# A mixture-of-experts kernel whose expert lists go from 96 slots to 128, in an order that goes around sixteen groups of partitions

## The reference

```python
def expert_block(args):
    tok, e = args
    xb = x_pad[tok]
    hb = jax.nn.silu(xb @ w_gate[e]) * (xb @ w_up[e])
    return hb @ w_down[e]
...
yb = yb.reshape(n_rows, dm) * row_w[:, None].astype(yb.dtype)
routed = jax.ops.segment_sum(yb, row_tok, num_segments=n_tok + 1)[:n_tok]
```

## Time and profile before

| | |
|---|---|
| median of 3 runs | 1192.11 us (1189.66 to 1192.6) |
| the profiled execution | 1189.86 us, its span 1188.1 us, mean granted clock 0.98 |
| PE busy (weight loads apart) | 94% of the span |
| PEld, DVE, ACT, POOL busy | 71%, 71%, 58%, 27% |
| experts | from about 450 to 1090 us of the span |
| DMA engines in that stretch | busy share at the top digit, 355 to 375 GB/s in most slices |
| DRAM traffic | 275 MB read, 36 MB written |

### The profile page before, as it was taken

One profiled execution on the slowest core, in us unless ns is written; L12 is line 12 of the kernel. 1 busy time (PEld: TensorE's weight loads), 2 busy tenths in 40 slices (PEclk: granted clock), 3 DMA queues, 4 the chain that ended last, 5 costly groups with the idle time before them and its releaser, 6 DMA issues.

```text
span 1188.1 us, 15715 instructions
## 1 busy us (share of the span) xinstructions
PE 1120.9 (94%) x5390; PEld 843.3 (71%) x5390; DVE 846.1 (71%) x1034; ACT 688.6 (58%) x692; POOL 326.0 (27%) x183
## 2 busy tenths in 40 slices
PE   2999999998999889999999999999999999999896
PEld 2878877777878665777777776767777777667475
DVE  7454345453444575999999988988989998887376
ACT  4431234342232432887888887777878887777344
POOL 4000000000002432444444443433444443331431
PEclk9999999998989999999999999999999999999899
DMA  7532222113234536999999999999999999998721
GB/s 284 169 105 71 71 71 70 38 36 142 73 118 175 211 111 233 348 365 373 368 375 368 368 369 355 364 357 353 363 364 358 370 371 358 363 363 266 244 110 54
DMA packets 68475, 294.78 MB, mean 248 GB/s; under 512 B 11216, under 2 KB 14288, under 8 KB 43600
## 3 DMA queue, kind: packets, MB, share of 16 engines
q1 hardware_dynamic: 52944, 256.43, 57.3%
q0 software_dynamic: 14912, 35.68, 12.2%
q10 hardware_dynamic: 576, 2.10, 0.5%
HBM read 275.29 MB, written 35.65 MB: 262 GB/s over the span
## 4 chain that ended last, share of the span: by engine, by line
PE 37%; DMA 16%; DVE 6%; ACT 3%; issue 3%; DVEq 0%; ACTq 0%; POOLq 0%; SPq 0%
DMA gu_raw<-in_moe_w_up 13%; PE ps L400 10%; PE ps L402 10%; PE ps L401 10%; PE ps L1454 3%; DVE w_lo L1653 2%; ACT w_hi L1545 2%; PE ps L1908 1%; PE ps L1194 1%; DMA gu_raw<-in_moe_w_gate 1%; DMA residual_rows<-y,put_idx 1%; DMA odd_rows<-y,put_idx 1%; PE ps L1478 1%; DVE w_lo L384 1%; PE ps L1445 1%
## 5 line engine op out<-in xcount | busy, mean ns | idle before, releaser
L1653 DVE TENSOR_TENSOR w_lo<-gu_raw,w_hi 128x2048 fp32r<-128x2048 f32 x126 | 288.5, 2290 | 52.0 <-ACT w_hi L1545 51.4
L1545 ACT ACTIVATE w_hi<-gu_raw 128x2048 fp32r<-128x2048 f32 x128 | 242.6, 1913 | 55.1 <-DMA gu_raw<-in_moe_w_up 42.9
L400 PE MATMUL ps<-w_hi,xgT_hi 128*96 128x512 f32 x512 | 205.9, 402 | 5.9 <-issue 3.2
L1756 POOL DMA_INDIRECT xg<-h_rows,get_idx x64 | 154.5, 2414 | 206.0 <-DVE get_idx L1641 156.5
L402 PE MATMUL ps<-w_hi,xgT_lo 128*96 128x512 f32 x512 | 202.9, 396 | 0.0
L401 PE MATMUL ps<-w_lo,xgT_hi 128*96 128x512 f32 x512 | 201.7, 394 | 0.0
L400 PE MATMUL ps<-w_hi,act_hi 128*128 128x512 f32 x384 | 156.4, 407 | 5.3 <-PEq L494 2.8
L401 PE MATMUL ps<-w_lo,act_hi 128*128 128x512 f32 x384 | 151.5, 394 | 0.0
L402 PE MATMUL ps<-w_hi,act_lo 128*128 128x512 f32 x384 | 151.4, 394 | 0.0
L1658 DVE TENSOR_TENSOR dn_lo<-dn_raw,dn_hi 128x2048 fp32r<-128x2048 f32 x64 | 146.0, 2282 | 4.3 <-ACT dn_hi L1551 4.1
L280 POOL TENSOR_TENSOR x_rows<-x_rows,ln_b 128x1024 f32<-128x1024 f32 x10 | 23.8, 2377 | 401.3 <-DVE x_rows L273 401.3
(11 more groups left out here) (201 smaller groups left out, 1740.6 us busy)
## 6 DMA issues: line engine op xcount, KB each, us to landing
gu_raw<-in_moe_w_gate SPq DMA_DIRECT2D x64, 1024.0 KB, 15.0
gu_raw<-in_moe_w_up SPq DMA_DIRECT2D x64, 1024.0 KB, 14.8
dn_raw<-in_moe_w_down SPq DMA_DIRECT2D x64, 1024.0 KB, 14.7
raw<-in_w_in SPq DMA_DIRECT2D x18, 1024.0 KB, 5.1
h_rows<-x_rows SPq DMA_DIRECT2D x8, 512.0 KB, 4.7
raw<-in_w_out SPq DMA_DIRECT2D x4, 1024.0 KB, 5.6
ple_raw<-in_ple_w_gate SPq DMA_DIRECT2D x4, 1024.0 KB, 10.5
x_rows<-in_x SPq DMA_DIRECT2D x4, 512.0 KB, 6.6
```

The costliest lines, as they stand in the source:

```text
L400: nc.tensor.matmul(out, x_hi, w_hi, start=first, stop=False)
L1545: nc.scalar.activation(m.w_hi[:, 2 * x.b + half], m.gu_raw[:, 2 * x.b + half], ACT.Copy).then_inc(gu_hi, 1)
L1653: nc.vector.tensor_tensor(m.w_lo[:, 2 * x.b + half], m.gu_raw[:, 2 * x.b + half], m.w_hi[:, 2 * x.b + half].bitcast(F32), ALU.subtract).th ...
L1756: nc.gpsimd.indirect_dma_start(out=m.xg[x.q][0:CAP], out_offset=None, in_=h1, in_offset=bass.IndirectOffsetOnAxis(ap=m.get_idx[x.q][0:CAP] ...
```

## The change

The list gets 128 slots, so that it covers all partitions. The `iota` into `slots` becomes two, which give another order: partition p = 64h + 32u + 4g + v (h, u of 0 and 1, g of 0 to 7, v of 0 to 3) holds the place 8h + g + 16u + 32v. The eight partitions that share h and g are one of sixteen groups; group 8h+g holds the places 8h+g, 8h+g+16, and so on. Two tiles move, because with 128 columns for each block they are larger: `hT_lo` to 110 KiB, `onehot` to 181 KiB. The number of rounds that the slots could need falls from 6 to 4; one is run either way.

```diff
-SLOTS = 96
+SLOTS = 128
 FAR = 4096.0
-QUEUES = 16
...
-        self.hT_lo = at("hT_lo", [P, 2, 2 * cap], F32R, 181)
+        self.hT_lo = at("hT_lo", [P, 2, 2 * cap], F32R, 110)
...
-        self.onehot = at("onehot", [P, 2, NT, cap], BF16, 182.5)
+        self.onehot = at("onehot", [P, 2, NT, cap], BF16, 181)
...
-    nc.gpsimd.iota(m.slots[:, 0:rounds * cap].rearrange("p (r q j) -> p r q j", r=rounds, q=QUEUES),
-                   pattern=[[cap, rounds], [1, QUEUES], [QUEUES, cap // QUEUES]], base=0, channel_multiplier=0,
-                   allow_small_or_imprecise_dtypes=True)
+    parts = m.slots[:, 0:rounds * cap].rearrange("p (r h u g v) -> p r h u g v", r=rounds, h=2, u=2, g=8)
+    for u in range(2):
+        nc.gpsimd.iota(parts[:, :, :, u], pattern=[[cap, rounds], [8, 2], [1, 8], [32, 4]], base=16 * u,
+                       channel_multiplier=0, allow_small_or_imprecise_dtypes=True)
```

## The result

The changed kernel takes 1199.23 us (median of 4 runs, 1198.66 to 1203.69) against 1191.23 us for the kernel before in the same comparison: ratio 1.0076, 95% interval 1.0047 to 1.0104. In a second comparison it came to 1.0099 (1.0064 to 1.0135). It is slower; the forecast was 1187.4 us, and faster. The profiled execution of after took 1203.69 us, its span 1202.0 us.

A forecast was written before the change was run, and what follows sets the result against it. The prediction took the engines to bound the early experts and the weight transfers the late ones. Early steps +3.2 us, late ones -8.9 and single items +1.0 gave -4.7, so 1187.4 us, range 1179 to 1200.

The forecast's parts named there:

- GpSimd: Making the transfer lists: at most 0.42 us more for 32 slots, hidden for gathers and counted as nothing for scatters.
- the cover: Slack before put_idx on DVE needs the scatter landed: step 0.14 us longer, put_idx about 0.4 us later in it.
- sign of being wrong: At put_idx on DVE: waits growing beyond some 5 us would show the prediction wrong.
- the scatter's lists: Rival, chance 0.05: GpSimd's delay grows, scatters land after put_idx wants them, 0.4 us in 60 steps, 1211 us.
- The transfers don't gain: Rival, chance 0.17: slow weight packets beside gathers come from two streams meeting, not from partitions; 1199 us.
- The transfers' relief: Expert weights and gathers on the DMA engines: 0.50 us less per expert, 0.03 us back for empty slots.
- The engines' pace: PE, DVE and ACT loop in the expert stage: 9.92 us a step, 0.14 more than 9.78.
- the engines take it all: Rival, chance 0.20: PE's matmul spacing stays at 0.232 us, engine pace 9.98 us a step, 1191.4 us.
- weight loads show: Rival, chance 0.03: 36 PE weight loads at +30 ns in the open, +1.1 us a step, 1252 us.
- The sum: Whole kernel: early steps +3.2 us, late ones -8.9, single items +1.0, together -4.7 us.

The follow-up runs named there:

- after_put4: The changed kernel with four put_idx tiles instead of two, so put_idx waits for the scatter of four experts back: 1179.92 us, ratio 0.9919 to the kernel before.
- after_same_chip: The changed kernel run once more, unaltered, beside the follow-up kernels on one chip: 1201.26 us, ratio 1.0099 to the kernel before.
- blocks128: The changed kernel with its 128 slots in the old kind of order, eight neighbouring partitions to a block: 1252.77 us, ratio 1.0543 to the kernel before.
- cols128: The kernel before, lists of 96 in the old order, with xgT, hT, onehot and their conversions 128 wide: ratio 1.0020.
- list128: The changed kernel's lists of 128 in the new order, but products, transposes and conversions for 96 columns: ratio 0.9974 to the kernel before.
- list128_put4: The changed kernel with products, transposes and conversions for 96 columns and four put_idx tiles: 1174.66 us, ratio 0.9877 to the kernel before.
- scat96: The changed kernel with put_idx and the scatter over partitions 0 to 95 alone, the gather keeping 128: ratio 0.9940 to the kernel before.

## Why the prediction was wrong, step by step

- **The step that failed is "GpSimd".** It had the right place and even the right wait, which it put at nothing, and its bound, "up to 0.4 us a step", is what the wait cost: 0.33 us early and 0.45 late, 19 to 21 us in all by the medians. Two terms were mis-sized. The landing was to go from 9.1 to 9.5 us; it is 10.1 at the median and 13.1 at worst in after_put4, and 10.7 and 13.3 in after_same_chip. Only the time in which GpSimd makes the list was priced there, and the way of the further slots through the DMA engines at 0.03 us, as a share of bandwidth. The packet records show the reverse: the time to the first packet stayed (5.2 and 5.1 us), and the packets' own stretch grew from 3.6 to 4.8. The other term is the cover, 0.14 and about 0.4 us: it grew by 0.2. And both were medians, while the latest landings went from 10.6 to 13.3 and 14.0 us, and a DVE wait is made by the late ones. A zero that rests on a cover of the same size as the cost was no zero. The prediction's own sign of being wrong, waits of `put_idx` beyond some 5 us, came: 26.1.
- **The rival that came true** had a chance of 0.05: the scatter's lists, with `put_idx` waiting. Its condition was that GpSimd's delay to the first packet grows, and that did not happen. Its result, 1211 us, is the forecast of 1187.4 with 0.4 us in 60 steps on top, 24 us. The wait cost 19 to 21, and what it stood on was lower than forecast (below).
- **The number 1199 stands in the prediction, by another rival.** "The transfers don't gain" (0.17) gave 1199 us, and 1199.23 was measured. That is luck: the transfers did gain, and a wait that this rival does not have took the gain back. The stated range, 1179 to 1200, holds the result for the same reason, and on the slower side.
- **The transfers' relief was right in kind and smaller than forecast**: 42.4 us of waits of ACT went. In the late windows the queues took of the sixteen engines, first before (692.1 to 1060.1 us), then in after_put4 (695.8 to 1053.2 us):

```profile
q1 hardware_dynamic: 15665, 114.10, 80.6%
q0 software_dynamic: 8064, 19.07, 21.4%
```

```profile
q1 hardware_dynamic: 15533, 113.11, 79.7%
q0 software_dynamic: 10368, 19.08, 21.4%
```

  Times the steps of 10.22 and 9.93 us, that is 10.43 and 10.04 us of all engines an expert, 0.39 us of relief, and 0.3 when the 0.9% more weight bytes in the first window are taken out; 0.50 - 0.03 was forecast. The rows of gathers fell to 159 ns as forecast (161). By blocks128 the relief needs the new order too, which the rows of the prediction could not tell. The gather's instruction on POOL is 0.39 us longer (2806 ns against 2414), hidden as forecast.
- **The engines' pace was right.** `onehot` 691 ns, `xgT_lo` 1218 ns in the rows above (0.69 and 1.21 forecast); without the wait the early steps take 9.91 us (9.92), the late ones 9.93 (9.98). PE's matmuls in the expert stage of after (738.10 to 742.42, 19 spacings) start 0.227 us apart:

```profile
738.10 0.39 PE L401 MATMUL ps<-w_lo,xgT_hi 128*128 128x512 f32 x1
...
742.42 0.40 PE L402 MATMUL ps<-w_hi,xgT_lo 128*128 128x512 f32 x1
```

  and not at 0.232 as in the earlier trace rows, in spite of the wider weight loads. The prediction left open whether the width or the load around it does that. It goes with the width: from 500 to 1060 us the spacings of these matmuls average 231.7 ns in before, cols128 and also list128 and list128_put4, which have the new transfers and 96 columns, and 228.0 to 228.2 in after, after_put4, blocks128 and scat96. Over 36 matmuls that is 0.13 us (0.12 taken). The rivals "the engines take it all" and "weight loads show" are out.
- **The sum** of -4.7 us, less the wait, was too small: after_put4 has -9.6 us (0.81% of 1190) where the same steps gave -4.7. The late steps at 9.93 in place of 9.98 account for 1.9 us of it; the other 3.0 stand against an interval of 2.3 us either way. In the profiles 2.7 us of it lie behind the late window (128.0 us before, 125.3 in after_put4, to the end of the span), where the prediction had +0.1; why is open.

## What to carry to other kernels

An empty slot of a transfer by list was cheap here in bandwidth and dear in latency: 32 more of them in a scatter added 0.8 us from its first packet to its last. When a list is widened, look first for who waits on its landing, and compare the cover with the latest landing in the trace, not the median. A wait that sits in the middle of a nearly full engine's queue delays everything behind it (here it cost half of its length to most of it); a few more bytes of index tiles took it away and turned +0.9% into -0.8%. When the number and the order of slots change together, try each alone where that can be done: here 128 slots in the old kind of order cost 5.4%, and in the new order, without the wait, they gained 0.8%. The new order was not tried with fewer slots.

## What the hardware showed that I had not expected

- A scatter over 128 slots in place of 96, with the same rows written, lands late enough to cost 1.1% of the kernel, under weight transfers that keep the engines busy. In the page of after, the 4096 further slots of 64 gathers and 64 scatters are 4096 more packets under 512 bytes (15312 against 11216). The DRAM counters nevertheless grow as if each were a row of 4 KB:

```profile
HBM read 283.67 MB, written 44.04 MB: 273 GB/s over the span
```

  against 275.3 and 35.65 MB before: 8.4 MB each, which is 2048 x 4096 bytes. The page of scat96, with only the gather widened, has 283.67 read and 35.65 written.
- The place of a list's rows among the partitions moved the traffic of all queues from 355 to 326 GB/s in the late window and the kernel by over 4% (blocks128 against after_same_chip).
- The float32r matmul with 128 stationary columns starts every 0.228 us on average and the one with 96 every 0.232, though its weight load takes 190 ns in after where the narrower takes 162.
